# Seven products of quarter sums for eight in the two down projections, with the weight sums added up in DRAM

## The reference

```
def swiglu(x, w_gate, w_up, w_down):
    return (jax.nn.silu(x @ w_gate) * (x @ w_up)) @ w_down
...
x = x + 0.5 * swiglu(rmsnorm(x, g_ffn1), w1_gate, w1_up, w1_down)
...
x = x + 0.5 * swiglu(rmsnorm(x, g_ffn2), w2_gate, w2_up, w2_down)
```

## Time and profile before

| what | before |
|---|---|
| time of three runs, us | 2003.36 (2003.04 to 2005.08) |
| span of the profiled execution, us | 2001.6 |
| TensorE busy | 1924.5 us (96%) |
| VectorE, ScalarE, GpSimd busy | 944, 549, 196 us |
| mean granted TensorE clock | 0.996 of full speed |
| moved by DMA | 358.7 MB |

### The profile page before, as it was taken

One profiled execution on the slowest core, in us unless ns is written; L12 is line 12 of the kernel. 1 busy time (PEld: TensorE's weight loads), 2 busy tenths in 40 slices (PEclk: granted clock), 3 DMA queues, 4 the chain that ended last, 5 costly groups with the idle time before them and its releaser, 6 DMA issues.

```text
span 2001.6 us, 24702 instructions
## 1 busy us (share of the span) xinstructions
PE 1924.5 (96%) x8909; PEld 1345.3 (67%) x8910; DVE 944.0 (47%) x1468; ACT 548.6 (27%) x840; POOL 196.0 (10%) x236
## 2 busy tenths in 40 slices
PE   8999999999997899997999999999999999999998
PEld 7888887884332233333788888886656688888886
DVE  4998983434111111113544443345796444444423
ACT  4234435341000000000522222233337642222222
POOL 2000000001111112111000000001237300000000
PEclk9999999999999999999999999999999999999999
DMA  6444232288999999999333322234110033333332
GB/s 206 151 138 126 85 100 90 84 365 315 425 425 426 427 426 395 421 426 373 94 96 101 97 94 95 93 98 108 60 54 5 12 95 95 94 94 107 102 96 74
DMA packets 153190, 358.70 MB, mean 179 GB/s; under 512 B 31756, under 2 KB 89537, under 8 KB 127898
## 3 DMA queue, kind: packets, MB, share of 16 engines
q1 hardware_dynamic: 147418, 349.64, 47.7%
q0 software_dynamic: 5680, 8.03, 1.1%
q10 hardware_dynamic: 16, 0.00, 0.0%
HBM read 348.29 MB, written 19.40 MB: 184 GB/s over the span
## 4 chain that ended last, share of the span: by engine, by line
PE 78%; SPq 8%; DVE 5%; DMA 4%; ACT 3%; issue 2%; POOL 1%; ACTq 0%; DVEq 0%
PE psum L508 15%; PE psum L510 15%; PE psum L509 15%; PE psum L1356 7%; SPq L1222 6%; PE psum L649 5%; PE psum L651 5%; PE psum L650 5%; PE psum L1366 3%; DMA expert_down_third<-in_w_expert_down_dram 2%; DMA arena<-in_w_expert_down_dram 2%; PE psum L2143 1%; PE psum L2176 1%; DVE arena L2498 1%; SPq L1225 1%
## 5 line engine op out<-in xcount | busy, mean ns | idle before, releaser
L503 DVE TENSOR_TENSOR w_lo<-w_raw,w_hi 128x1024 fp32r<-128x1024 f32 (+1 forms) x232 | 286.9, 1236 | 567.1 <-ACT w_hi L498 567.0
L508 PE MATMUL psum<-h_hi,w_hi 128*128 128x512 f32 x1240 | 488.1, 394 | 3.9 <-DVE h_lo L990 1.9
L510 PE MATMUL psum<-h_hi,w_lo 128*128 128x512 f32 x1240 | 483.4, 390 | 0.0
L509 PE MATMUL psum<-h_lo,w_hi 128*128 128x512 f32 x1240 | 483.1, 390 | 0.0
L498 ACT ACTIVATE w_hi<-w_raw 128x1024 fp32r<-128x1024 f32 (+1 forms) x232 | 245.1, 1056 | 862.1 <-PE psum L510 644.3
L508 PEld LDWEIGHTS psum<-h_hi,w_hi 128*128 128x128 f32 x1240 | 233.2, 188 | 56.7 <-issue 5.2
L509 PEld LDWEIGHTS psum<-h_lo,w_hi 128*128 128x128 f32 x1240 | 233.4, 188 | 49.4 <-issue 1.7
L510 PEld LDWEIGHTS psum<-h_hi,w_lo 128*128 128x128 f32 x1240 | 233.1, 188 | 48.8
L1356 PE MATMUL psum<-arena,w_raw 128*64 128x512 f32 x800 | 181.7, 596 | 13.4 <-DMA arena<-in_w_expert_up_dram 12.5
L1018 DVE SCALAR_TENSOR_TENSOR arena<-arena,vec 128x512 f32<-128x512 f32 x240 | 162.7, 752 | 1.0 <-ACT arena L845 1.0
L1491 ACT ACTIVATE w_raw<-psum 128x256 f32<-128x256 f32 x36 | 13.8, 383 | 461.7 <-PE psum L1356 461.7
(11 more groups left out here) (341 smaller groups left out, 2050.9 us busy)
## 6 DMA issues: line engine op xcount, KB each, us to landing
arena<-in_w_expert_gate_dram SPq DMA_DIRECT2D x44, 1024.0 KB, 23.3
arena<-in_w_expert_up_dram SPq DMA_DIRECT2D x44, 1024.0 KB, 26.2
arena<-in_w_expert_down_dram SPq DMA_DIRECT2D x22, 2048.0 KB, 28.9
w_raw<-in_w_in_dram SPq DMA_DIRECT2D x44, 512.0 KB, 3.7
w_raw<-in_w_gate_dram SPq DMA_DIRECT2D x88, 256.0 KB, 2.8
w_raw<-in_w_up_dram SPq DMA_DIRECT2D x88, 256.0 KB, 3.0
w_raw<-in_w_down_dram SPq DMA_DIRECT2D x44, 512.0 KB, 3.6
expert_down_third<-in_w_expert_down_dram SPq DMA_DIRECT2D x10, 2048.0 KB, 28.0
```

The lines of the kernel that those rows point to most:

```text
L503: eng.tensor_tensor(wlo[:, s, :, 0:n], raw[:, slot, :, 0:n], whi[:, s, :, 0:n].bitcast(F32), ALU.subtract).then_inc(w_lo, 1)
L508: eng.matmul(o, w_h, x_h, start=first, stop=False)
L509: eng.matmul(o, w_h, x_l, start=False, stop=False)
L510: return eng.matmul(o, w_l, x_h, start=False, stop=last)
```

## The change

Both operands of the down product are cut in quarters: the token activations by halves of the tokens (256) and by even and odd tiles of the 2816 inner rows (e = 0, 1), the weights by even and odd row tiles and by halves of the 1024 columns. Seven products of such quarters, or of sums of quarters, are computed in place of eight (`PRODUCTS`), and the results are put together by additions. A product has 11 row tiles in 6 chunks, the last with one tile; a chunk has 2 token tiles x 2 row tiles x 3 parts, 12 matmuls.

- The sums of activations (`s1`, `s2`, `s4`, and one in place) are made by GpSimd in `pool_ffn`, 4 operations of 128x256 for each of the 11 groups, behind each group of gate and up.
- The sums of weights are made in DRAM buffers by `pool_terms`: 4 plain and 4 adding transfers of a quarter (2.9 MB), 6 DMAs each, from GpSimd's queue. Those of the first feed-forward layer are issued right behind `pool_block1`, those of the second ahead of the token sums of the first.
- The activations are kept unsplit; ScalarE and VectorE split them chunk by chunk in the down stage, beside the weights. A third slot for split chunks lies in `h_lo`.
- VectorE reads PSUM for two token tiles at once, and `kept` holds a sum of products that goes to three quarters of the result. The last product gives the second column half of token tiles 0 and 1 only, so the order of the last rows is 2, 3, 0, 1.
- Several pairs of semaphores become one with a higher count, to make room; the order of the events they count is as it was.

```diff
-C_UP = [72, 166]
+C_UP = [72, 186]
...
+PRODUCTS = ("A11B11", "S3T3", "A12B21", "S2T2", "A22T4", "S1T1", "S4B22")
+QUARTERS = {0: (0, 0), 2: (1, 0), 6: (1, 1)}
+TERM_OF = {1: 0, 3: 1, 4: 2, 5: 3}
+N_CH = (N_UP + 1) // 2
+N_DN = len(PRODUCTS) * N_CH
+DSLOTS, TERMS = 3, 16 * 8 * N_CH
...
         def sp_ffn(sp, j):
...
+            sp.wait_ge(terms_r[j], TERMS)
+            for x in range(N_DN):
+                prod, m = x // N_CH, x % N_CH
+                sp.wait_ge(w_lo, C_DN[j] + x - RAW + 1)
+                sp.dma_start(raw[:, (C_DN[j] + x) % RAW, 0:pair_size(m), :], weights_of(down, j, prod, m)).then_inc(
+                    w_raw[(C_DN[j] + x) % RAW], 16)
...
+        def pool_terms(pool, j):
...
+            def term_dma(n, src, step=None):
+
+                for m in range(N_CH):
+                    pool.dma_start(term(j, n, m), src(m), accum_op=ALU.bypass if step is None else ALU.add).then_inc(
+                        terms_r[j], 16)
...
+            term_dma(0, quarter(0, 1))
+            term_dma(1, quarter(0, 0))
+            term_dma(2, quarter(1, 0))
+            term_dma(3, quarter(0, 1))
+            pool.wait_ge(terms_r[j], 4 * N_CH * 16)
+            term_dma(0, quarter(1, 1), 1)
+            term_dma(3, quarter(0, 0), 1)
+            pool.wait_ge(terms_r[j], 6 * N_CH * 16)
+            term_dma(1, lambda m: term(j, 0, m), 1)
+            pool.wait_ge(terms_r[j], 7 * N_CH * 16)
+            term_dma(2, lambda m: term(j, 1, m), 1)
+
+        def pool_ffn(pool, j):
+
+            def token_sums(g, i=0):
...
+                pool.tensor_tensor(a21, a11, a21, ALU.subtract).then_inc(sums_r, 1)
+                pool.wait_ge(sums_r, n + 1)
+                pool.tensor_tensor(s2[:, k, :], a22, a21, ALU.add).then_inc(sums_r, 1)
+                pool.wait_ge(sums_r, n + 2)
+                pool.tensor_tensor(s4[:, k, :], s2[:, k, :], a12, ALU.subtract).then_inc(sums_r, 1)
+                pool.tensor_tensor(s1[:, k, :], s2[:, k, :], a11, ALU.subtract).then_inc(sums_r, 1)
+
+            if j == 0:
+                pool_terms(pool, 1)
+            token_sums(0)
+            token_sums(1)
...
         def pe_ffn(pe, j):
...
+            banks = (4, 6, 0, 2, 4, 0, 2)
+            group_read(pe, G_DN[j] - 2)
+            for x in range(N_DN):
...
+                pe.wait_ge(w_lo, C_DN[j] + x + 1)
+                pe.wait_ge(dx_lo, N_DN * j + x + 1)
...
+                for a, t in order:
+                    f, o = slice(t * P, t * P + P), psum[:, banks[prod] + t, :]
+                    begin, end = m == 0 and a == 0, m == N_CH - 1 and a == n - 1
+                    pe.matmul(o, x_h[:, a, f], w_h[:, a, :], start=begin, stop=False)
+                    pe.matmul(o, x_l[:, a, f], w_h[:, a, :], start=False, stop=False)
+                    mm = pe.matmul(o, x_h[:, a, f], w_l[:, a, :], start=False, stop=end)
...
         def act_ffn(act, j):
...
+            for x in range(N_DN):
...
+                act.wait_ge(w_used, C_DN[j] + (x - 1 if x < SPLIT else x - 2 if x >= DSLOTS else 0))
+                act.activation(w_h, raw_of_down(j, x), ACT.Copy).then_inc(w_hi, 1)
...
+                act.activation(x_h, operand_of(x), ACT.Copy).then_inc(dx_hi, 1)
+                if x == 2:
+                    gate(N_UP - 1)
+                if x == N_CH + 2:
+                    act.wait_ge(w_used, C_DN[j] + N_CH)
+                    act.activation(kept, psum[:, 4:6, :], ACT.Copy, scale=0.5).then_inc(first_kept, 1)
+                if x == 5 * N_CH + 4:
                     square_half(act, 1 + 2 * j, 0, range(TT))
-                if j == 0 and n == N_UP + 3:
+                if j == 0 and x == 6 * N_CH + 4:
+                    act.wait_ge(w_lo, C_DN[0] + 6 * N_CH)
                     turned_high(act, 5, 4, gain_of("g_mix_2"), range(4))
...
         def dve_ffn(dve, j):
...
-                products_hi(g - 1, i)
-                products_lo(g - 1, i)
...
+            def after(x):
+
+                if x == 2:
+                    products(N_UP - 1)
...
+                if x == N_CH + 3:
+                    add_bank(N_CH, 4, both(0, 0)).then_inc(joined, 1)
...
+                if x == 4 * N_CH + 2:
+                    dve.wait_ge(w_used, C_DN[j] + 4 * N_CH)
+                    dve.wait_ge(first_kept, j + 1)
+                    dve.scalar_tensor_tensor(out=kept, in0=psum[:, 2:4, :], scalar=-0.5, in1=kept, op0=ALU.mult,
+                                             op1=ALU.add).then_inc(joined, 1)
+                if x == 4 * N_CH + 3:
+                    join(both(2, 0))
+                if x == 4 * N_CH + 4:
+                    join(both(2, 1), ALU.subtract)
+                if x == 4 * N_CH + 5:
+                    join(both(0, 1), ALU.subtract)
...
+                if j == 0 and x == 6 * N_CH + 4:
+                    turned_low(dve, 5, 4, gain_of("g_mix_2"), range(4))
...
+            for x in range(N_DN):
+                w_h, w_l, x_h, x_l = down_slots(x)
+                if x == 2:
+                    scaled(N_UP - 1)
+                dve.wait_ge(w_hi, C_DN[j] + x + 1)
+                dve.tensor_tensor(w_l, raw_of_down(j, x), w_h.bitcast(F32), ALU.subtract).then_inc(w_lo, 1)
+                dve.wait_ge(dx_hi, N_DN * j + x + 1)
+                dve.tensor_tensor(x_l, operand_of(x), x_h.bitcast(F32), ALU.subtract).then_inc(dx_lo, 1)
+                after(x)
...
         def dve_last(dve):
...
+            normed(0, 2)
+            normed(1, 3)
+            last_rows()
+            normed(2, 0)
+            normed(3, 1)
...
             pool_block1(pool)
+            pool_terms(pool, 0)
             pool_moe(pool)
+            pool_ffn(pool, 0)
             pool_mix(pool)
+            pool_ffn(pool, 1)
```

More of the change, by code:

```diff
@@ L474, in first_group @@
                 if k == 0:
-                    ready()
-                    turn_half(eng, bt, 1)
+                    turn_half(eng, bt, 1, ready, LAST_ROWS if n == 5 else range(TT))
                 if k == spread_at:
@@ L1776, in program, with pair_size, down_weights, weight_quarter @@
         diag = ar3[:, 24576:25088]
+        kept = sq_[:, :].rearrange("p (t n) -> p t n", t=2)
         row_junk = ar3[:, 8192:9216]
         over_root = stat_std[:, :].unsqueeze(1).to_broadcast([P, 2, T])
+        def pair_size(m):
+            return min(CK, N_UP - CK * m)
+        def down_weights(j):
+            return A[f"w{j + 1}_down_2"].rearrange("o (k e p) n -> p e (o k) n", e=2, p=P)
+        def weight_quarter(down, m, e, half):
+            return down[:, e, CK * m:CK * m + pair_size(m), half * CN:half * CN + CN]
+        def term(j, n, m):
+            return terms[j][n][:, CK * m:CK * m + pair_size(m), :]
+        def weights_of(down, j, prod, m):
+            if prod in QUARTERS:
+                return weight_quarter(down, m, *QUARTERS[prod])
+            return term(j, TERM_OF[prod], m)
+        def raw_of_down(j, x):
+            return raw[:, (C_DN[j] + x) % RAW, 0:pair_size(x % N_CH), :]
+        def operand_of(x):
+            prod, m = x // N_CH, x % N_CH
+            ks, first, second = slice(CK * m, CK * m + pair_size(m)), slice(0, HALF_T), slice(HALF_T, T)
+            return (act[:, ks, 0, first], act[:, ks, 0, second], act[:, ks, 1, first], s2[:, ks, :],
+                    act[:, ks, 1, second], s1[:, ks, :], s4[:, ks, :])[prod]
+        def down_slots(x):
+            s, n = x % DSLOTS, pair_size(x % N_CH)
+            third = hlo_[:, 4 * T:8 * T].rearrange("p (f k n) -> p f k n", f=2, k=CK)
+            high, low = (whi[:, s], wlo[:, s]) if s < SPLIT else (third[:, 0], third[:, 1])
+            return high[:, 0:n, :], low[:, 0:n, :], dxh[:, s, 0:n, :], dxl[:, s, 0:n, :]
         def sp_ffn(sp, j):
@@ L1968, in dve_ffn, with both @@
                     group(g, i, 8)
[L1969 to L1984 removed]
+            def both(t, half):
+                return rows_tok[:, t:t + 2, half * HALF:half * HALF + HALF]
@@ new lines, in last_rows @@
+            def last_rows():
+                for t in range(2):
+                    if t == 0:
+                        dve.wait_ge(row_done, 2 * (TT - 1) * (j + 1) + j + 1)
+                    else:
+                        dve.wait_ge(w_used, C_DN[j] + N_DN)
+                    rows = rows_tok[:, t, HALF:D]
+                    dve.scalar_tensor_tensor(out=rows, in0=psum[:, 2 + t, :], scalar=-0.5, in1=rows, op0=ALU.mult,
+                                             op1=ALU.add).then_inc(evac[(G_DN[j] + 1) % 2] if t else x1_r, 1)
```

302 lines of the change are left out of this document (170 added, 132 removed).

## The result

The changed kernel took 2008.75 us (median of 7 runs, 2006.30 to 2013.16); the kernel before took 2003.36 us in 7 runs beside it (2001.48 to 2005.08). The ratio is 1.0029 with a 95% interval of [1.0019, 1.0039]: **slower by 5.4 us**, where 8.9 us less had been forecast. The time lies inside the range and on the other side of zero.

What follows compares the result with a forecast made beforehand. TensorE, busy 96% of the span, was taken to bound the kernel. Terms -29.9 + 8.5 + 1.5 + 6 + 3 + 2 = -8.9 us gave 1994.5 us from 2003.4; own range 1986 to 2001, whole range 1978 to 2018.

Steps and rivals of the forecast that it cites:

- The products: Down projections: 462 matmuls in place of 528 a stage, at 0.2266 us each, gain 29.9 us in the two stages.
- What feeds them: Down stages: splitting operands and weights for shorter chunks makes TensorE wait, 8.5 us given back in all.
- The waits at chunks 1 and 3: Start of each down stage: TensorE waits 0.6 us at chunk 1 and 1.7 us at chunk 3 for low parts.
- The one at chunk 2: Start of each down stage: VectorE scales the last gate before chunk 2's lows, so TensorE waits 0.4 us.
- the one at product 5: Down stage: VectorE's splitting and joins in product 4 exceed TensorE's time, leaving a wait of 0.9 us.
- The end: End of the kernel: the last square comes at TensorE's end + 3.8 us, 1.5 us given back (bounds -1 and +3).
- First gate and up: First gate and up: 1-KB load packets share engines with adds priced at 0.15 us; 3 us lost.
- The rival of starved adds: First gate and up: adds starve the chunk loads, slower than before, 2022 us at 0.25 us an add; chance 0.19.
- The seam: After the experts: the second stage's transfers delay loads up to the first gate and up chunk, 6 us (bounds 0 and 13).
- The first block: First block: same transfers beside 0.44 DMA share and a nearly full VectorE, 2 us lost (bounds 0 and 8).
- the transfers hide entirely: Whole kernel: queues in advance cover the weight-sum transfers, -19.9 us, 1983.5 us; chance 0.30.
- The rival of slow feeding: Down stages: loads landing late or handovers above 0.1 us add 5.5 us a stage, 2005 us; chance 0.13.

Runs made afterwards that it cites:

- experiment 10: First sums as in experiment 6, second as in experiment 8; VectorE does the last group's product behind chunk 3, not chunk 2, of the down stage: 1980.76 us, single run.
- experiment 9: First sums as in experiment 6, second as in experiment 8, plus three more rounds of a 2.9 MB adding transfer beside the second stage's sums: 1979.03 us, single run.
- experiment 2: Changed kernel, with GpSimd waiting until the router weights have landed before it issues the first stage's weight sums: 2001.91 us, 0.9990.
- experiment 5: As experiment 3, with SyncE's router loads moved from chunk 10 to behind chunk 40 of the first block and VectorE's use to chunk 48: 1982.33 us, 0.9893.
- experiment 6: As experiment 4, with GpSimd also waiting for the gain rows before the first stage's weight sums: 1980.61 us, 0.9886.
- experiment 3: Changed kernel, with GpSimd issuing the second stage's weight sums only after TensorE has done the first group of gate and up: 1996.05 us, 0.9965.
- experiment 7: As experiment 4, but the first stage's weight sums wait until TensorE has done 36 chunks, some 215 us: 1981.20 us, 0.9887.
- experiment 8: As experiment 7, but the second stage's weight sums start once the first chunk of gate and up is split: 1979.75 us, 0.9884.
- experiment 4: Changed kernel with both delays, that of experiment 2 for the first stage's sums and that of experiment 3 for the second's: 1990.54 us, 0.9937.

## Why the prediction was right in part and wrong in sum

**The products: right.** 462 matmuls a stage at 0.227 us. The term of -29.9 with its own costs, 8.5 and 1.5, made -19.9; experiment 1, which has the products and none of the transfers, measured -22.3.

**What feeds them: right in kind, too dear by half a stall.** The waits at chunks 1 and 3 came where the prediction put them. By the distance between matmul starts they cost 0.6 and 1.8 us, against 0.6 and 1.7 in the text. The one at chunk 2 (0.4) and the one at product 5 (0.9) didn't come. Before the mix it was 0.9, against 1.15. In all 5.7 us, not 8.5. Experiment 10 shows the cause of the largest. That its size was met is in part luck: 0.5 of its 1.8 us is an operation of VectorE that took 1.21 us in place of 0.68 (below), which the text did not have.

**The end: right in kind.** From TensorE's end to the last square were 3.0 us, against 2.5 before and 3.8 in the text. From TensorE's end to that of the span it is 0.6 us more than before, not 1.5.

**First gate and up: nothing, where 3 was taken.** The row of 62% above, and experiment 9, show it. The price of an add was close. A packet's time is 16 engines x stretch x share / packets. The copies took 16 x 45 x 0.715 / 3200 = 0.161 us for 3.6 KB. The adds took 0.168 us for 1.9 KB (84 to 130 us: 3005 packets, 5.76 MB, 68.4%), beside 0.15 in the text. So an add moves about half as much per engine and us as a copy, 11 KB against 22. The Trainium skill (Collectives: The Full Stack, "The bandwidth ceiling: the fold count and why AG ≠ RS ≠ AR") says the same of the adding step of a collective, since the addition needs two source reads. The trace agrees with the rate. But the prediction's sum gave 12.5 us at 0.198, twice its price of a 2-KB copy; with the 0.168 us measured its sum gives 352 x 0.221 - 75.8 = 2.0 us, and not even this appeared. The rival of starved adds (0.19) is refuted. (Its price, 2022, lay outside the stated range up to 2018, too.)

**The seam: right in kind, half of its size.** 6 us was taken, between 0 and 13; it measured 11.5. The working let one packet of the second queue pass for each of the load's own, at 0.099 us, the time of a 2-KB packet. The copies went in packets of 3.6 KB on average, 200 an engine in place of the 352 of the text, and such a packet takes 0.161 us: by the same count 67 packets an engine x 0.161 = 10.8 us, against the 10.9 by which the landing moved. The mis-sized term is the time of one packet of a DRAM-to-DRAM copy. The last 0.6 us lie behind the landing, where the clock is lower (0.77 in 960 to 990 us, behind the 12.6 us of idle time, against 0.94 in 930 to 960). That the queues take turns one for one was read from a gather at 0.45 us a packet; this is 1.6 of the 0.282-us packets beside it and not "one to one and a half", so the agreement of 10.8 with 10.9 is closer than the rule deserves.

**The first block: this is the step that failed.** "The same transfers beside 0.44 DMA share and a nearly full VectorE: bounds 0 and 8, I take 2." It measured 13.6, above the bound. These 11.6 alone turn the sum of -8.9 to +2.7; the other misses (5.5 more in the seam, 3 less in gate and up, 2.8 less in the stalls, 0.9 less at the end) nearly cancel, which is luck. The step asked what share of the engines was free. It did not ask what stands in SyncE's queue at that moment, in what order, and how long each takes to issue. For the seam the load was followed packet by packet; for the first block the text has no row of SyncE's queue. It would have shown two loads that take 3.78 and 3.51 us to issue, with no second queue at all, where a chunk's takes 0.4. An issue that takes eight times as long as another is one to suspect when a second queue is to fill the engines. (The engines were busy to 0.90 in 45 to 50 us and to 0.59 in 50 to 55 even then, above the 0.44 of the whole stretch that the text went by.) Experiments 2, 5 and 6 show it from three sides: delay the copies past those loads, move those loads, or delay the copies past the gain row too, and 6.8, 13.7 and 15.4 us go (5 and 6 against experiment 3). An estimate with the prediction's own rule of turns would have shown the size: the two weight loads of the router have 1024 rows each in DRAM, 64 packets an engine, and each of these behind one copy packet of 0.161 us makes 10.3 us a load, beside the 11.57 and 11.00 us that the two issues behind them took.

Put together: -29.9, +5.7, +0.6, +11.5, +13.6 make +1.5, where the two spans show +2.9. The 1.4 left over lies mostly in the two down stretches (0.8 and 0.5 less gained than matmuls and waits say) and was not followed further.

**The rivals.** That the transfers hide entirely (1983.5) is what experiments 5 to 8 reach, 1979.75 to 1982.33, once they start at another moment. The rival of slow feeding named 2005, near the time measured, by a mechanism that the trace doesn't show: chunk loads of the down stage were never late.

What stays open: why a load of 2 KB takes 11 us to issue. That an issue waits until the packets of the loads ahead of it in its own queue have gone, each in turn with the other queue's, fits the rows: in experiments 2 and 4 the gain row's loads are issued in under 1 us each, and the chunks behind them take 2 to 5. But no run varied the number of packets, so this is argued and not shown.

## What to carry to other kernels

Before new transfers are put beside a stage, read the issuing queue's own timeline for that stage: loads of tiny packets that took 3.5 to 3.8 us to issue here took 11 to 12 beside a full second queue, and everything behind them in that queue was late. The mean share of free engines did not tell this. Start background transfers behind the last small load, and behind the first load of the next stage that nothing covers: one wait each was worth 28 us of 2009 here (experiment 6). In the steady part of a stage with chunks in advance, DMA engines filled to twice their former share cost nothing here.

## What the runs showed of the hardware

- Issuing a load from SyncE took many times as long beside a full second queue: 0.37 to 0.47 us for half a chunk became up to 5 us (where tiny packets stood ahead of it; else it stayed), 3.51 became 11.00 for 2 KB of router bias, 1.36 became 10.31 for the two loads of the gain row. The Trainium skill (DMA: Bandwidth & Descriptors, "Issuing engines are not separate DMA queues") calls the time to initiate a DMA usually small relative to the DMA itself; here it was not small (11.00 of the 23.8 us to the landing of the 2-KB load), and it decided the time.
- An adding transfer from DRAM to DRAM took 0.168 us for a packet of 1.9 KB and 0.274 us for one of 3.4 KB (132 to 153 us: 843 packets, 2.86 MB, 68.7%), a copy 0.161 us for 3.6 KB.
- GpSimd issued a copy of 256 to 512 KB from DRAM to DRAM in 0.67 us (24 in 16.06) and an adding one in 0.84 to 1.12 (6 in 5.02, 12 in 13.48), against the 1.05 us of a gather that the prediction took.
- While GpSimd made the last token sums (1232.84 to 1238.43 us), VectorE's operation on 128x512 took 1.21 us where it takes 0.68 else. Its timeline in the changed kernel:

```profile
1233.81 1.21 DVE L2181 TENSOR_TENSOR down_operands<-products,down_operands 128x512 fp32r<-128x512 f32 x1
...
1243.31 0.68 DVE L2181 TENSOR_TENSOR down_operands<-products,down_operands 128x512 fp32r<-128x512 f32 x1
```

This lies right ahead of chunk 3, and no term of the prediction had it. In experiment 10 the token sums start at 1210.25 us, and there the slower operation is the one at 1211.23 (1.22 us): it moves with them. That they cause it is not shown further.
